# Second block's attention on one NeuronCore: the product with V by 128-query tiles, one turn behind the probabilities, with two score buffers in place of three

## What is computed, cut to what matters

```
q: 512 queries, 4 heads of 128;  k, v: 512 + 256 = 768 keys, 2 heads of 128 (two q heads share one)
s = q @ k.T * 128**-0.5
p = softmax(s)            # over the 768 keys
attn = p @ v              # 512 x (4 heads * 128)
x = x + gt1 * (concat([attn, conv]) @ w_out)
```

## Time and profile before

| what | value |
|---|---|
| median of the three runs | 2527.57 us |
| the profiled execution's own time | 2525.92 us |
| its span in the trace | 2524.1 us |
| busy share of the span: PE, DVE, ACT, POOL | 96%, 81%, 52%, 27% |
| attention, from the first scores to the start of the output projection | 1128.09 to 1197.28 us |
| one turn's DVE work: L946, L948, L937, L939 (mean) | 0.16, 0.69, 0.96, 0.15 us |
| one turn's ACT work: L817 with its read of the sum, L850 (mean) | 0.90 and 0.20, 0.81 us |
| DMA in the attention stage | 2% of the 16 engines' time |

### The profile page before, as it was taken

How to read it: one execution, slowest core, us unless ns; L and a number is a source line. 1 busy time by engine, 2 the same in 40 slices (tenths; PEclk the granted TensorE clock), 3 DMA queues, 4 the chain that set the end, 5 groups by cost and what they waited for, 6 DMA issues and landing times.

```text
span 2524.1 us, 31372 instructions
## 1 busy us (share of the span) xinstructions
PE 2420.9 (96%) x10771; PEld 1934.3 (77%) x10771; DVE 2036.4 (81%) x1844; ACT 1319.5 (52%) x1206; POOL 683.3 (27%) x407
## 2 busy tenths in 40 slices
PE   8999999999999999998869999999999999999995
PEld 7777778786877787874657888888888888888884
DVE  7788587576885786884259999999999999999994
ACT  4442223334323244334327777777777777777772
POOL 5333341342423432340221222122112211221120
PEclk9999999999999999999969999999999999999998
DMA  6232245222422652220049999999999999999992
GB/s 236 83 130 71 75 152 174 67 76 78 139 67 82 257 211 69 75 93 1 13 177 372 367 373 366 378 365 372 368 371 370 373 361 380 361 372 368 375 358 96
DMA packets 104426, 572.47 MB, mean 227 GB/s; under 512 B 14192, under 2 KB 14336, under 8 KB 54288
## 3 DMA queue, kind: packets, MB, share of 16 engines
q1 hardware_dynamic: 86784, 515.15, 53.9%
q0 software_dynamic: 17280, 56.20, 7.7%
q10 hardware_dynamic: 288, 0.14, 0.0%
HBM read 559.37 MB, written 24.12 MB: 231 GB/s over the span
## 4 chain that ended last, share of the span: by engine, by line
PE 89%; DVE 6%; ACT 2%; issue 1%; DVEq 1%; DMA 1%; ACTq 0%; SPq 0%; POOLq 0%
PE ps L1479 85%; PE ps L1157 2%; DVE scr L2180 1%; DVE y_split L2117 1%; PE ps L665 0%; DVE mix L2231 0%; DVE scr L2229 0%; DMA mix<-acc_rows 0%; DVE scr L948 0%; DVEq L2127 0%; PE ps L701 0%; DMA acc_rows<-rows,lst 0%; DVE w_split L1284 0%; PE ps L1409 0%; DVE hT L2377 0%
## 5 line engine op out<-in xcount | busy, mean ns | idle before, releaser
L1284 DVE TENSOR_TENSOR w_split<-raw,w_split 128x2048 fp32r<-128x2048 f32 x386 | 877.3, 2287 | 54.6 <-ACT w_split L1236 43.5
L1479 PE MATMUL ps<-y_split,pieces_split 128*128 128x512 f32 x3600 | 846.9, 396 | 19.6 <-POOLq L2547 7.8
L1236 ACT ACTIVATE w_split<-raw 128x2048 fp32r<-128x2048 f32 x386 | 736.1, 1916 | 197.8 <-PE ps L1479 178.2
L1479 PEld LDWEIGHTS ps<-y_split,pieces_split 128*128 128x128 f32 x3600 | 681.9, 190 | 172.4 <-issue 29.0
L1479 PE MATMUL ps<-w_split,rows_T 128*128 128x512 f32 x3096 | 752.2, 394 | 1.9 <-DVE rows_T L1290 1.9
L1479 PEld LDWEIGHTS ps<-w_split,rows_T 128*128 128x128 f32 x3096 | 575.5, 188 | 119.4 <-DVE rows_T L1290 2.5
L2535 POOL TENSOR_TENSOR pieces_split<-pieces,pieces_split 128x1024 fp32r<-128x1024 f32 x151 | 373.2, 2482 | 653.5 <-ACT pieces_split L1813 524.9
L1813 ACT ACTIVATE pieces_split<-pieces 128x1024 fp32r<-128x1024 f32 x144 | 151.3, 1058 | 434.5 <-PE ps L1479 403.2
L1479 PE MATMUL ps<-w_split,hidden_T 128*128 128x512 f32 x1536 | 363.7, 392 | 1.7 <-DVE hidden_T L1290 1.7
L1479 PEld LDWEIGHTS ps<-w_split,hidden_T 128*128 128x128 f32 x1536 | 285.8, 188 | 72.5 <-DVE hidden_T L1290 13.5
L1348 POOL COPY rows_i<-slot_tokens 128x1 int32 (+1 forms) x34 | 59.5, 1750 | 407.7 <-PE ps L1157 374.0
(11 more groups left out here) (265 smaller groups left out, 2074.9 us busy)
## 6 DMA issues: line engine op xcount, KB each, us to landing
raw<-in_w_moe SPq DMA_DIRECT2D x386, 1024.0 KB, 7.5
pieces<-in_pieces SPq DMA_DIRECT2D x181, 512.0 KB, 3.6
scr<-in_ada POOLq DMA_DIRECT2D x48, 512.0 KB, 5.4
scr<-in_ple SPq DMA_DIRECT2D x2, 1536.0 KB, 7.0
acc_rows<-in_zeros POOLq DMA_DIRECT2D x5, 512.0 KB, 10.9
hT<-in_xT SPq DMA_DIRECT2D x8, 256.0 KB, 5.5
h_rows<-scr SPq DMA_DIRECT2D x4, 512.0 KB, 3.5
mix<-acc_rows SPq DMA_DIRECT2D x4, 512.0 KB, 5.1
```

The source lines that it names most:

```text
L1236: nc.scalar.activation(wsp[:, p % SPLIT, 0], raw[:, p % RAW, :], ACT.Copy).then_inc(high, 3 if p == 1 else 1)
L1284: nc.vector.tensor_tensor(wsp[:, p % SPLIT, 1], raw[:, p % RAW, :], wsp[:, p % SPLIT, 0].bitcast(F32), ALU.subtract).then_inc(low, 3 if p ...
L1479: return pe.matmul(out, lhsT, rhs, start=start, stop=stop)
```

## The change

The product with V is made for each tile of 128 queries in a function of its own, `attended(n)`, which PE issues one turn after the tile's transposes. Its results go to banks 6 and 7 in turn (`o_tile`). Bank 6 and 7 were the third score buffer, so two score buffers are left, and `scores(n + 2)` now waits for the exponential of turn n. The transposes no longer wait for the output of the head before. DVE copies each 128x128 result (`o_out`), two turns behind its own loop. Waits on `o_ready` count tiles in place of heads.

```diff
@@ -503,11 +503,14 @@
         be_ready, np_ready = sem("be_ready"), sem("np_ready")
         onehot_ready, onehot_used, list_ready, acc_init = sem("onehot_ready"), sem("onehot_used"), sem("list_ready"), sem("acc_init")
 
-        SCORE_BANK = (0, 2, 6)
+        SCORE_BANK = (0, 2)
 
         MIXED = (4, 5, 6, 7, 0, 1, 2, 3)
         ATT_SCALE = float(P) ** -0.5
         SH1, SC1, GT1, SH2, SC2, GT2 = range(0, 48, 8)
+
+        def o_tile(n):
+            return ps[:, 6 + n % 2, 0:P]
 
         def tail_sp(sp):
             for t in range(A_RAW, len(TAIL)):
@@ -648,9 +651,9 @@
             pe.wait_ge(qkv_done, 1)
 
             def scores(n):
-                h, t, b = n // ST, n % ST, SCORE_BANK[n % 3]
-                if n >= 3:
-                    pe.wait_ge(exp_ready, n - 2)
+                h, t, b = n // ST, n % ST, SCORE_BANK[n % 2]
+                if n >= 2:
+                    pe.wait_ge(exp_ready, n - 1)
                 q = qTa[:, h, t * P:(t + 1) * P]
                 mm(ps[:, b, :], q, kTa[:, h // 2, 0:S], True, True)
                 mm(ps[:, b + 1, 0:CTX], q, kTa[:, h // 2, S:KEYS], True, True).then_inc(sc_full, 1)
@@ -660,11 +663,20 @@
                 if n >= 1:
                     pe.wait_ge(pt_ready, n)
                 for j in range(KT):
-                    if j == 4 and n % ST == 0 and n:
-                        pe.wait_ge(o_ready, n // ST)
                     m = pe.transpose(ps[:, 4 + j // 4, (j % 4) * P:(j % 4 + 1) * P],
                                      prob[:, n % 2, j * P:(j + 1) * P], ident[:])
                 m.then_inc(pt_full, 1)
+
+            def attended(n):
+
+                h, t = n // ST, n % ST
+                pe.wait_ge(pt_ready, n + 1)
+                if n >= 2:
+                    pe.wait_ge(o_ready, n - 1)
+                for j in range(KT):
+                    m = mm(o_tile(n), vall[:, j, (h // 2) * P:(h // 2 + 1) * P], eT[:, j, t * P:(t + 1) * P],
+                           j == 0, j == KT - 1)
+                m.then_inc(o_full, 1)
 
             scores(0)
             scores(1)
@@ -672,13 +684,10 @@
                 if n + 2 < QH * ST:
                     scores(n + 2)
                 turned(n)
-                if n % ST == ST - 1:
-                    h = n // ST
-                    pe.wait_ge(pt_ready, n + 1)
-                    for j in range(KT):
-                        m = mm(ps[:, 5, :], vall[:, j, (h // 2) * P:(h // 2 + 1) * P], eT[:, j, :], j == 0, j == KT - 1)
-                    m.then_inc(o_full, 1)
-            pe.wait_ge(o_ready, QH)
+                if n >= 1:
+                    attended(n - 1)
+            attended(QH * ST - 1)
+            pe.wait_ge(o_ready, QH * ST)
             pe.wait_ge(conv_ready, 4)
             for m_ in range(DK):
                 features(CV, f"w{m_}", f"w{m_}", ys, order=MIXED, rows_ready=mixl if m_ == 0 else None)
@@ -812,7 +821,7 @@
                 act.wait_ge(max_ready, n + 1)
                 if n >= 2:
                     act.wait_ge(pt_full, n - 1)
-                b, c = SCORE_BANK[n % 3], 16 + n % 3
+                b, c = SCORE_BANK[n % 2], 16 + n % 3
                 s_ = ps[:, b:b + 2, :].rearrange("p a b -> p (a b)")[:, 0:KEYS]
                 nc.scalar.activation(prob[:, n % 2, :], s_, ACT.Exp, bias=small[:, c:c + 1],
                                      scale=ATT_SCALE, accum_out=small[:, c + 3:c + 4]).then_inc(exp_ready, 1)
@@ -822,10 +831,10 @@
                     act.wait_ge(conv_ready, 4)
                     mixed_high(7)
                 if n > ST and n % ST == 2:
-                    act.wait_ge(o_ready, n // ST)
+                    act.wait_ge(o_ready, n // ST * ST)
                     mixed_high(n // ST - 1)
             turned_copy(act, QH * ST - 1)
-            act.wait_ge(o_ready, QH)
+            act.wait_ge(o_ready, QH * ST)
             mixed_high(QH - 1)
             ahead(T_AT["w3"])
 
@@ -931,13 +940,18 @@
                     conv_step(i, step)
 
             def rows_max(n):
-                b, c = SCORE_BANK[n % 3], 16 + n % 3
+                b, c = SCORE_BANK[n % 2], 16 + n % 3
                 dve.wait_ge(sc_full, n + 1)
                 s_ = ps[:, b:b + 2, :].rearrange("p a b -> p (a b)")[:, 0:KEYS]
                 nc.vector.reduce_max(small[:, c + 6:c + 7], s_, AX.X)
                 dve.drain()
                 nc.vector.tensor_scalar(small[:, c:c + 1], small[:, c + 6:c + 7], -ATT_SCALE, None,
                                         ALU.mult).then_inc(max_ready, 1)
+
+            def o_out(n):
+                h, t = n // ST, n % ST
+                dve.wait_ge(o_full, n + 1)
+                nc.vector.tensor_copy(mix[:, 8 + h, t * P:(t + 1) * P], o_tile(n)).then_inc(o_ready, 1)
 
             rows_max(0)
             rows_max(1)
@@ -952,10 +966,10 @@
                     rows_max(n + 2)
                 if n < 4:
                     conv_step(3, n)
-                if n % ST == ST - 1:
-                    h = n // ST
-                    dve.wait_ge(o_full, h + 1)
-                    nc.vector.tensor_copy(mix[:, 8 + h, :], ps[:, 5, :]).then_inc(o_ready, 1)
+                if n >= 2:
+                    o_out(n - 2)
+            o_out(QH * ST - 2)
+            o_out(QH * ST - 1)
 
             dve.sem_inc(CV.free, len(CV.banks))
             dve.sem_inc(CA.free, len(CA.banks))
```

## The result

The changed kernel takes 2514.95 us in the median of five runs (2514.28 to 2516.70), against 2527.57 us before (2526.86 to 2530.43). The medians are 12.6 us apart. The measured ratio is 0.9946, with a 95% interval of 0.9933 to 0.9959, which is 10 to 17 us, so it is faster. 2515.7 was forecast.

A forecast was written before the change was run, and what follows sets the result against it. The engines took turns in a 69.2 us attention stage; filling PE's waits saves 16.4 - 3.7 - 0.8 = 11.9 us, giving 2515.7 us for the median. Its own range was 2511 to 2520, the 8-in-10 range 2510.5 to 2523.

The forecast's parts named there:

- The bound: Attention stage: the moved product fills PE's gaps; PE needs 3.35 us a turn, 53.6 us for 16 turns.
- The product of a tile: On PE: 12 instructions of 128 columns at 0.112 us, 1.34 us a tile; the split costs 0.8 us over the stage.
- The two score buffers cost nothing: Scores waiting for the exponential of turn n have 2.9 us to spare; the wait binds only at the start, costing nothing.
- The tightest place: From scores to next transposes through DVE: 3.8 us, due after 4.66 us, leaving 0.9 us to spare.
- The end: Last turns: the 3.8 us loop binds once, at transposes(14); the output projection starts at 1185.39, 11.9 us earlier.
- The clock: Last head's product: 1.7 us of slow clock counted as saved; rival: clock falls for the stage, about 2565 us, chance 0.03.
- The port: DVE's normalisings beside POOL's splits: if each of four splits held one up, 1.5 us lost, total 2517; not adopted.
- The total: Whole kernel: median of 2515.7 us, from 2527.57 us, by starting the output projection 11.9 us earlier.
- a turn paced by DVE: Rival in the attention loop: steps late beyond the 0.9 us slack stall PE each turn; 2521 us, chance 0.13.
- The weight loads: Rival at PE's 48 load-and-matmul pairs a head: loads not overlapped, 0.214 us a pair, 2534.9 us; chance 0.06.
- The loss behind the stage: Rival: the gain is lost after the attention stage, total about 2527 us; chance 0.04.

The follow-up runs named there:

- e4: Changed kernel with each tile's product made twice, 12 more instructions a turn: 2536.76 us in one run, stage 77.40 us.
- e7: Kernel before, with a head's product split into four tiles of 128 queries at its old place: 2529.38 us in one run, stage 69.93 us.
- e2: Kernel before, with two score buffers in place of three: 2527.04 us in one run, stage 67.99 us.
- e5: Changed kernel with one idle reduction over 512 columns added on DVE each turn: 2517.76 us in one run, stage 61.28 us.
- e11: e5 with the splits of the heads moved behind the loop: 2516.18 us in one run, stage 58.54 us.
- e6: Changed kernel with three idle reductions added on DVE each turn, some 1.8 us: 2532.16 us in one run, stage 72.78 us.
- e9: Kernel before, with DVE's output of a head moved behind the next head's first normalising: 2525.72 us, ratio 0.9989, stage 66.60 us.
- e3: Changed kernel with the product made by pairs of tiles, 256 queries at once: 2520.63 us, ratio 0.9973, stage 63.50 us.
- e1: Changed kernel with each tile's product in its own turn, right behind its transposes: 2535.11 us, ratio to before 1.0026, stage 75.87 us.
- e8: Changed kernel with the last convolution's steps in turns 4 to 7 and its rows' splits in the loop: 2513.62 us, ratio 0.9952.
- e10: e8 with the convolution's steps in turns 6, 7, 8 and 10 and its fourth split in turn 12: 2515.37 us, ratio 0.9953.

## Why the prediction was right

Step by step, by its own numbers:

- **The bound.** PE is busy for all of the 41.6 us from 1137.05 to 1178.70. Shown by e4: doubling the product adds its whole price.
- **The product of a tile, 1.34 us.** Turn 3.29 us, forecast 3.35; e4 gives 1.34 for 12 instructions, e7 0.2 us a head for the split. The transposes were set 0.04 us high (0.66), the scores 0.02 (1.29). In the last products, back to back, an instruction took 0.112 us as well (e7); the lower bound of 0.107 was not reached in any of these rows.
- **The two score buffers cost nothing.** One wait for an exponential at the start, 1.0 us long, hidden as said, since transposes(0) and (1) come where they came before after the first scores. e2 shows 0.5 us without the cover.
- **The tightest place, 0.9 us to spare.** 0.94 on the timeline from the normalising's end, and 0.59 a turn later, where DVE stood 0.43 us for nothing that the trace names. e5 and e11 hid 0.6 in it, e6 with 1.8 did not. But the sum left something out: in turns 2 and 3 DVE also has a step of the last convolution, 0.74 and 0.68 us. There only 0.11 and 0.16 us were left (normalising's end 1143.57, transposes 1143.68; 1146.81 and 1146.97). That these turns cost nothing was luck, and e5 lost its first part there.
- **The end.** transposes(14) came 0.41 us later than PE's own work would have let them (0.26 of it idle in the trace), forecast as 0.45. The stage ended 56.43 us after it began, against 57.3 forecast: eleven turns of 0.06 us too much, 0.7, and 0.2 behind them. So 12.76 us were saved where 11.9 were forecast.
- **The clock.** The row of 0.53 is gone. But e2 and e9, with nearly the same waits before the last product, had no slow start either (12 instructions in 5.42 us), while e7 had (granted 0.61). The 1.7 us were therefore in part the luck of the one profiled execution, and the prediction booked them as a saving. The stage's gain by order alone is nearer 11 us.
- **The port.** The sum of 2517 did not come: 15 of 16 normalisings took 0.62 us. It had assumed that each split would meet a normalising, and none of the four in the loop did. The mechanism, however, is there (last section).
- **The total.** 2514.95 came within 0.8 us of 2515.7. That closeness is in part luck: the stage saved 0.9 us more than forecast, 1.7 us of its saving may not belong to the edit, and 1.4 were lost behind it. The interval of the ratio is over 3 us to either side. The terms are confirmed by the stage's rows, not by the total.

Of the rivals, a turn paced by DVE did not come, but e3 and e6 show it at work once the cover or the slack is gone. (The 16 waits that spoke for it were the weight loads'; PE's matmuls themselves waited in 10 turns.) The weight loads stayed hidden. The rule in the Trainium skill ("TensorE: Matmul & The Clock Gate", Part 3), that a load overlaps a running matmul only in other row groups, is not what these float32 matmuls of 128 columns do: a load, 0.19 us long by itself, and a matmul came every 0.112 us, on the full array; the same Part's other case, a load into the background weight buffer, would fit, but nothing here shows which buffer it was. The clock stayed at 1.00 in all four windows. The loss behind the stage was 1.4 us, not all.

## What to carry to other kernels

When several engines hand one tile round, look for a lump of work on the bounding engine that leaves the others idle, cut it to the size of a turn and issue it one turn late. Both halves are needed here: the cut without the delay was slower than the start (e1; and e7, at the old place, by 0.7 us of stage), and larger lumps with the delay left half of the gain by the totals (e3). The delay with no cut at all was not run. A third buffer given up for that costs little where the wait it brings stands in front of a wait that exists anyway. And once a loop runs with 0.9 us to spare, and less in the turns that carry other work, look at what else shares a port with the engine in the loop before adding or moving anything.

## What the runs showed of the hardware

A 128x768 float32 tensor_scalar on DVE took 0.62 us alone and 1.65 to 1.70 us where a POOL tensor_tensor of 1.27 us ran beside it; in e8 POOL began 0.03 us earlier, in e5 in the same hundredth. The added 1.0 to 1.1 us are most of POOL's 1.27, and in each of these meetings, the first turn's too, the normalising ended 0.41 or 0.42 us after POOL's instruction. The other order is in e5 as well: a split that began at 1149.57, while the normalising of 1149.42 ran, took 1.60 us, and the normalising 0.62. In the changed kernel, after its first turn, POOL began at most 0.09 us before the normalising ended and nothing was lost. e5 against e11 and e8 against e10 show it by taking the meeting away. The Trainium skill ("SBUF — State Buffer", Who interferes with whom) says that the later one to ask for the port pair waits for the whole instruction of the other; these runs agree, in both orders. What was not expected is how a small shift decides it: the changed kernel escaped the meeting in every turn but the first, by an order that nobody had set for it.
